# Router fed from the transposed layer result, paired ring slots, and 44 matmuls on constants behind the mixer

## Chip, cores and metric

One core of one Trainium2 chip. The metric is the device time of one execution in microseconds (us). The kernel before takes 895.5 us (median of 3 runs, 894.67 to 897.81). All matrices are float32.

## What is computed

One layer (DEPTH 1) on 320 tokens (256 of a prompt, 64 of 8 samples), model width 2048, 16 experts of width 512 in 4 groups:

```python
def token_mixer(x, ...):
    h = einsum('btd,de->bte', x, w_in)                 # 2048 -> 4352 columns
    b_gate, c_gate, h_conv, u, v, p = split(h, cuts)
    y_conv = b_gate * short_conv(c_gate * h_conv)      # causal, width 3
    y_chunk = u * chunk_mix(layer_norm(v), w_s, b_s)
    y_pool = pool_w(trailing_mean(p) - p) * pool_scale
    return einsum('bte,ed->btd', concat(y_conv, y_chunk, y_pool), w_out)
x = layer_norm(ALPHA * x + token_mixer(x))             # its argument is z below
# router: group logits x @ rg_w (4), expert logits x @ re_w (16); one group, two of its four experts
a = silu(x @ w_gate[e]) * (x @ w_up[e]) * combine[e]
x = layer_norm(ALPHA * x + sum_e a @ w_down[e])
```

## The kernel before, in words

The program is written for the five engines by hand, with semaphores; each engine runs its list in order, and SyncE (SP) issues nearly all loads.

**Mixer.** Both projections run in chunks of 8 x 128 rows by 256 columns of weights (1 MB): 34 chunks of `w_in` (17 groups of two), then 16 of `w_out` (groups 17 to 24, `G_O` = 17), 50 in all (`CHUNKS1`). A chunk c is loaded to `raw[c % 3]`, ScalarE writes its rounded part `w_hi` (`split_hi`), VectorE the remainder `w_lo`, into the place of `raw` (`split_lo`), and TensorE runs 48 matmuls on it (`group_products`) and raises `w_used`. SP issues chunk c when `w_used` is c - 2, so a load has the time of two chunks less the two splits. PSUM holds three pairs of banks, one for each group in turn. The activations stand transposed in SBUF: `xT_hi`, `xT_lo`, later `yT_hi`, `yT_lo` (the latter from `y_lo`, L817). The second half of group 17 waits for the last of these.

**End of the mixer.** For each group k of 256 output columns ScalarE copies the pair of banks to `mixT` (L794), TensorE transposes it back to rows of tokens (`out_tokens`, six transposes, L625 and L630), VectorE adds `ALPHA * x` from `tok` into `tok` (`residual`, L983 and L988) and takes statistics (L997). `store_z` writes `tok` to `z_rows` in DRAM, columns of groups 0 to 5 from ACT's queue, those of 6 and 7 from SP's. After the last group `pe_router` transposes `tok` once more (`turn_z`, L1147, 48 transposes), ScalarE evicts to `zT` (L1370), `route` multiplies it by the router's weights scaled with the norm's gain (L1155), two matmuls on `sums` and `rbias` (L1170, L1171) give the norm's correction, and three with `fold` (L1176) turn the logits to rows. VectorE then works out the selection in small operations (L1460 to L1550), from which come `row` (the first group's tokens; L1464) and `facts`. GpSimd gathers the first expert group's rows from `z_rows` (L1108) when `row` is known and `z_rows` is whole; `info` (L1205) reads `facts`; VectorE builds `order`, `gated` and the next `group_slot` (L1557) and normalises the gathered rows (`xg`, L1589); `fill` (L1220) transposes them, ScalarE evicts with gain and bias (L1390), and `gate_up` (L1284) begins.

**Experts.** Each expert is 6 units of 2 MB: four of gate and up (`gu_w`) and two of down (`down_w`), 96 in all. Units 0 to 4 are loaded during the mixer (`load_half`), units 5 to 10 in `sp_experts` between the mixer's end and the first `gate_up`; every later one, from 11 (`FIRST`), waits for `ring_used`, which TensorE raises with each unit it has used; `gate_up(0, 0)` is the first. SP's list is in order, and so are its loads. At the end comes the last group's norm and its scatter.

## Time and profile before

| | |
|---|---|
| median of 3 runs | 895.5 us |
| profiled execution: device time | 897.55 us |
| profiled execution: span of its instructions | 895.7 us |
| PE busy | 838.7 us, 94% |
| DVE, ACT, POOL busy | 282.4, 263.8, 24.8 us |
| DMA | 267.80 MB, mean 299 GB/s |
| mean granted TensorE clock | 0.979 of 2.4 GHz |

The span is cut by the profile into 40 slices of 22.4 us; the mixer is the first 17.6 of them, the router's stage about 1.5, the experts the rest. "PEld" is TensorE's weight load, "SPq" is SP's queue of DMA issues. A row of a timeline gives the start, the duration, the engine with its line in the kernel, the tiles written and read, and the count where rows were merged; in square brackets the idle time of that engine just before and what ended it. float32 matmuls show twice in a count.

### The profile page before, as it was taken

What the parts mean: (1) busy time and instruction counts of PE and PEld (TensorE: products, weight loads), DVE (VectorE), ACT (ScalarE), POOL (GpSimd) and SP (SyncE); (2) the same over time, 40 slices, a digit from 0 to 9 for tenths busy, and PEclk for the clock granted to TensorE, in tenths of its full rate; (3) what the DMA queues carried; (4) which work ended last, traced back from release to release, by engine and by line L of the source; (5) the groups of instructions that cost most, each with busy time, mean ns of one, the idle gap of its engine ahead of it and who ended that gap; (6) DMA issues with size and microseconds to landing.
All of it is one profiled execution on the core that took longest, in us unless ns stands there. A gap on an engine that the chain in (4) does not pass through costs nothing.

```text
span 895.7 us, 11202 instructions
## 1 busy us (share of the span) xinstructions
PE 838.7 (94%) x4729; PEld 558.7 (62%) x4729; DVE 282.4 (32%) x390; ACT 263.8 (29%) x465; POOL 24.8 (3%) x41
## 2 busy tenths in 40 slices
PE   6999999999999999995989999999999998897993
PEld 6989999999999999983433334433333333333331
DVE  6273384434764435355000102043003220022203
ACT  5234232322233323312432332432223322133101
POOL 0000000000001000001000000000000100000000
PEclk8999999999999999996899999999999999999997
DMA  9643553665444774459898999999999999999980
GB/s 298 185 142 120 188 164 127 192 205 164 144 140 153 282 282 141 141 220 384 353 426 351 421 423 422 428 418 423 424 425 420 424 426 420 422 424 425 421 355 37
DMA packets 81149, 267.80 MB, mean 299 GB/s; under 512 B 5626, under 2 KB 58320, under 8 KB 59657
## 3 DMA queue, kind: packets, MB, share of 16 engines
q1 hardware_dynamic: 78042, 258.92, 74.6%
q0 software_dynamic: 1984, 5.31, 1.5%
q10 hardware_dynamic: 1078, 2.94, 1.0%
q8 instruction: 33, 0.54, 0.2%
q14 instruction: 12, 0.09, 0.0%
HBM read 263.07 MB, written 11.54 MB: 307 GB/s over the span
## 4 chain that ended last, share of the span: by engine, by line
PE 68%; DMA 18%; DVE 6%; ACT 3%; SPq 2%; issue 2%; POOL 0%; POOLq 0%; ACTq 0%; DVEq 0%
PE ps L1284 16%; PE ps L476 12%; PE ps L477 12%; PE ps L478 12%; DMA gu_w<-in_expert_w_up 7%; PE ps L1318 6%; DMA down_w<-in_expert_w_down 4%; DMA xg<-z_rows,row 3%; PE ps L1220 3%; DMA out<-xg,sample_row 3%; SPq L398 2%; ACT xT L1390 1%; PE ps L529 1%; DVE xg L1639 1%; PE ps L1261 1%
## 5 line engine op out<-in xcount | busy, mean ns | idle before, releaser
L1284 PE MATMUL ps<-gu_w,xT 128*64 128x512 f32 x1024 | 235.3, 601 | 14.7 <-DMA gu_w<-in_expert_w_up 13.7
L657 DVE TENSOR_TENSOR w_lo<-raw,w_hi 128x2048 fp32r<-128x2048 f32 x50 | 114.5, 2291 | 173.5 <-ACT w_hi L649 171.9
L1284 PEld LDWEIGHTS ps<-gu_w,xT 128*64 128x64 f32 x1024 | 72.6, 138 | 142.5 <-issue 136.4
L476 PE MATMUL ps<-xT_hi,w_hi 128*128 128x320 f32 x512 | 159.2, 311 | 0.0
L477 PE MATMUL ps<-xT_lo,w_hi 128*128 128x320 f32 x512 | 158.3, 309 | 0.0
L478 PE MATMUL ps<-xT_hi,w_lo 128*128 128x320 f32 x512 | 158.2, 309 | 0.0
L649 ACT ACTIVATE w_hi<-raw 128x2048 fp32r<-128x2048 f32 x49 | 93.8, 1915 | 210.0 <-DMA raw<-in_w_in 138.1
L1390 ACT ACTIVATE xT<-ps,gbT 128x64 f32<-128x64 f32 x256 | 82.2, 406 | 158.7 <-PE ps L1220 158.7
L1318 PE MATMUL ps<-down_w,aT 128*64 128x512 f32 x480 | 106.5, 596 | 0.6
L1661 DVE TENSOR_TENSOR a_sb<-ps,a_sb 128x256 f32<-128x256 f32 x16 | 6.8, 424 | 289.4 <-ACT a_sb L1444 289.4
L476 PEld LDWEIGHTS ps<-xT_hi,w_hi 128*128 128x128 f32 x512 | 96.1, 188 | 0.5
L477 PEld LDWEIGHTS ps<-xT_lo,w_hi 128*128 128x128 f32 x512 | 96.1, 188 | 0.0
L478 PEld LDWEIGHTS ps<-xT_hi,w_lo 128*128 128x128 f32 x512 | 96.1, 188 | 0.0
L476 PE MATMUL ps<-yT_hi,w_hi 128*128 128x320 f32 x256 | 79.8, 312 | 0.9 <-DVE yT_lo L817 0.9
L478 PE MATMUL ps<-yT_hi,w_lo 128*128 128x320 f32 x256 | 79.1, 309 | 0.0
L477 PE MATMUL ps<-yT_lo,w_hi 128*128 128x320 f32 x256 | 79.1, 309 | 0.0
L1318 PEld LDWEIGHTS ps<-down_w,aT 128*64 128x64 f32 x480 | 33.0, 137 | 69.9 <-issue 59.3
L1220 PEld LDWEIGHTS ps<-order,xg 128*128 128x128 f32 x256 | 33.8, 195 | 54.3 <-issue 47.1
L1220 PE MATMUL ps<-order,xg 128*128 128x128 f32 x256 | 45.6, 304 | 5.4 <-DVE xg L1589 5.4
L476 PEld LDWEIGHTS ps<-yT_hi,w_hi 128*128 128x128 f32 x256 | 48.1, 188 | 1.2 <-DVE yT_lo L817 1.1
L477 PEld LDWEIGHTS ps<-yT_lo,w_hi 128*128 128x128 f32 x256 | 48.1, 188 | 0.0
L478 PEld LDWEIGHTS ps<-yT_hi,w_lo 128*128 128x128 f32 x256 | 48.1, 188 | 0.0
(261 smaller groups left out, 523.4 us busy)
## 6 DMA issues: line engine op xcount, KB each, us to landing
gu_w<-in_expert_w_gate SPq DMA_DIRECT2D x64, 1024.0 KB, 15.3
gu_w<-in_expert_w_up SPq DMA_DIRECT2D x64, 1024.0 KB, 19.0
down_w<-in_expert_w_down SPq DMA_DIRECT2D x32, 2048.0 KB, 24.1
raw<-in_w_in SPq DMA_DIRECT2D x34, 1024.0 KB, 5.3
raw<-in_w_out SPq DMA_DIRECT2D x16, 1024.0 KB, 5.4
tok<-in_x_prompt SPq DMA_DIRECT2D x2, 1024.0 KB, 6.0
z_rows<-tok ACTq DMA_DIRECT2D x2, 768.0 KB, 4.1
tok<-in_x_sample SPq DMA_DIRECT2D x1, 512.0 KB, 9.1
```

Source lines behind the costliest of these rows:

```text
L398: sp.dma_start(gu_w[s][:, n, :].rearrange("p (c f) -> p c f", c=4), src[:, e, h, c:c + 4, :])\
L476: pe.matmul(out, wh[:, t, col], hi[:, kt, :], start=(n == 0 and t == 0), stop=False)
L477: pe.matmul(out, wh[:, t, col], lo[:, kt, :], start=False, stop=False)
L478: last = pe.matmul(out, wl[:, t, col], hi[:, kt, :], start=False, stop=(n == 1 and t == CK - 1))
L529: last = pe.transpose(ps[:, n % 8, P * t:P * t + m], tok[0:m, i, 4 * q + t::KT], ident[0:m, 0:m])
L649: act.activation(w_hi[k][:, :], raw[k][:, :], ACT.Copy).then_inc(hi_ready, 1)
L657: dve.tensor_tensor(w_lo[k][:, :], raw[k][:, :], w_hi[k][:, :].bitcast(FP32), ALU.subtract)\
L1220: last = pe.transpose(ps[:, fill_bank(e, j), P * c:P * (c + 1)], xg[g % 2][:, col:HD * (j // 2 + 1):HK], order[:, k, :])
L1261: last = pe.matmul(ps[:, ACC + 2 * h + q, :], gatedT[half, k, :], y[half, 512 * q:512 * (q + 1)], start=(k == 0), stop=(k == EG - 1))
L1284: last = pe.matmul(ps[C * side:C * (side + 1), GU, :], x, w[:, :, c, FH * side:FH * (side + 1)], start=(j == 0 and c == 0), stop=(j == PAI ...
L1318: last = pe.matmul(ps[C * side:C * (side + 1), out + q, :], turned[:, f % 2, f // 2, :], down_w[slot(i)][:, n, col:col + 512], start=(f == ...
L1390: last = act.activation(xT[e % 2][:, j, c, :], ps[:, fill_bank(e, j), P * c:P * c + C], ACT.Identity, bias=gbT[:, 1, j // 2, hc:hc + 1], s ...
```

## The change

Buffers: `raw`/`w_lo` and `w_hi` of a ring slot now lie side by side, so that a slot is one 16 KB piece, and expert units take other places; `slot_at` names them. The rows of `w_in` and of x's transposes are taken as `(t p)` instead of `(p t)`, as those of `w_out` are.

Result: `mixT`, `out_tokens`, `residual`, `turn_z`, the eviction to `zT` and `store_z` go. GpSimd adds `xT_hi` and `xT_lo` into `x_all` (four operations of 128 x 1280, from `w_used` 34). VectorE makes `zt = ALPHA * x_all + ps` (`make_zt`), transposed, and both the router (`route`, for groups 0 to 5 inside the output projection) and the transposes to rows (`rows_of`, in the middle of the next group) read it. ScalarE copies the rows to `z_part` (`copy_rows`) and stores each group's 256 columns itself (`store_rows`); statistics come from `z_part` (`row_sums`). The last group's second half runs column by column. The router's weights are loaded by SP behind chunk 8 in the `(t p)` order, the norm's gain and bias with single elements as runs, and `router_weights` runs in group 18.

Loads: units 5, 6 and 7 are issued at `w_used` 48, `zt_ready` 7 and `w_used` 49, units 8 and 9 at `w_used` 50, unit 10 as before behind `raw_made` and the second `xg` clear.

TensorE: `keep_busy` issues 14, 3, 3, 9 and 15 matmuls 128x128 on `ident` and `slots` into a bank that nobody reads, at five places behind the mixer. The two copies of `vrstd` and `norm_bias` to `facts` move behind `gexp_in`.

```diff
...
-    RING_HI = RAW0 + 24 * KB
-    EARLY0 = RING_HI + 24 * KB
+    EARLY0 = RAW0 + 48 * KB
...
-    raw = [at(f"raw{s}", RAW0 + s * 8 * KB, [P, CH]) for s in range(3)]
-    slot_at = [EARLY0, EARLY0 + 16 * KB, T0 + 32 * KB, T0, T0 + 16 * KB, RAW0 + 16 * KB, RAW0 + 32 * KB,
-               YT_HI0 + 22 * KB, TOK0, RAW0, XA + 24 * KB]
+    raw = [at(f"raw{s}", RAW0 + s * 16 * KB, [P, CH]) for s in range(3)]
+    slot_at = [EARLY0, EARLY0 + 16 * KB, TOK0, TOK0 + 16 * KB, TOK0 + 32 * KB, RAW0 + 32 * KB, XA, RAW0,
+               YT_HI0 + 22 * KB, RAW0 + 16 * KB, XA + 24 * KB]
...
+    x_all = at("x_all", XA, [P, KT, NTOK])
+    zt = [at(f"zt{s}", LATE + s * 2 * ROW, [P, 2, NTOK]) for s in range(3)]
+    z_part = [at("z_part0", XA + 4 * XT_B, [P, 3, GW]), at("z_part1", XA + XT_B, [P, 3, GW])]
...
-    win_v = w_in[0].rearrange("(p t) n -> p t n", t=KT)
+    win_v = w_in[0].rearrange("(t p) n -> p t n", p=P)
...
+            if c == 8:
+                sp.wait_ge(x_full, 12)
+                sp.dma_start(rg_nat[:, :, :], rg_w[0].rearrange("(t p) n -> p t n", p=P)).then_inc(rw_in, 16)
+                sp.dma_start(re_nat[:, :, :], re_w[0].rearrange("(t p) n -> p t n", p=P)).then_inc(rw_in, 16)
+                for k, src in enumerate((ln1_g, ln1_b)):
+                    sp.dma_start(gb_nat[:, k, :], src[0].rearrange("(t p) -> p t", p=P),
+                                 allow_slow_non_contiguous=True).then_inc(gb_nat_in, 16)
+            if c in (12, 16, 20, 24, 28, 32):
...
-            if 4 <= o < 10:
-                if o == 4:
-                    sp.wait_ge(w_used, 2 * G_O)
+            if 6 <= o < 10:
                 if o == 6:
                     sp.wait_ge(ylo_ready, 7)
                     sp.wait_ge(small_out, 16 * (4 + NB))
-                load_half(sp, 2 + (o - 4) // 2, o % 2)
+                    sp.wait_ge(sums_ready, 2)
+                load_half(sp, 3 + (o - 6) // 2, o % 2)
...
+        if free:
+            pe.wait_ge(*free)
...
+            if n and by_column:
+                for f in range(2):
+                    out, col = ps[:, 2 * pair + f, 0:NTOK], slice(P * f, P * (f + 1))
+                    for t in range(CK):
+                        kt = CK * halves[n] + t
+                        pe.matmul(out, wh[:, t, col], hi[:, kt, :], start=False, stop=False)
+                        pe.matmul(out, wh[:, t, col], lo[:, kt, :], start=False, stop=False)
+                        last = pe.matmul(out, wl[:, t, col], hi[:, kt, :], start=False, stop=(t == CK - 1))
+                    last.then_inc(w_used if f else first_column, 1)
+                continue
...
-        def out_tokens(k, turn=0):
...
+        def route(tiles):
+            for kt in tiles:
+                j = kt % RQ
+                last = pe.matmul(ps[RP * j:RP * (j + 1), LGB, 0:NTOK], rw[:, kt, :], zt[kt // 2 % 3][:, kt % 2, :],
+                                 start=(kt < RQ), stop=(kt >= KT - RQ))
+            return last
+        def rows_of(k, columns):
+            for f in columns:
+                pe.wait_ge(zt_ready, k + 1 + (f if k == 7 else 0))
+                if f == 0:
+                    if k == 0:
+                        wait_read(pe, "z0", "z1")
+                    else:
+                        pe.wait_ge(rows_read, 3 * k)
+                for i in range(2):
+                    pe.transpose(ps[:, ROWB, GW * i + P * f:GW * i + P * (f + 1)],
+                                 zt[k % 3][:, f, P * i:P * (i + 1)], ident[:, :])
+                out, samples_of = ps[64 * f:64 * (f + 1), 2 * ((G_O + k) % 3), NTOK:NTOK + P], zt[k % 3][:, f, SEQ:NTOK]
+                if f == 0:
+                    last = pe.transpose(out, samples_of, ident[:, :])
+                else:
+                    last = pe.matmul(out, samples_of, ident[:, :], start=True, stop=True)
+            return last
+        def behind(k):
+            def step(n):
+                if n != CK - 1:
+                    return
+                rows_of(k, (0, 1)).then_inc(rows_made, 1)
+                if k % 2:
+                    if k == 1:
+                        pe.wait_ge(rw_ready, 4)
+                    route(range(2 * k - 2, 2 * k + 2)).then_inc(zt_used, 1)
+                if k == 6:
+                    pe.wait_ge(sums_ready, 2)
+                    pe.wait_ge(rbias_in, 32)
+                    out = ps[:, 3, 0:2 * NR]
+                    pe.matmul(out, ones[:, :].bitcast(FP32), sums[:, :, :].rearrange("p k n -> p (k n)"),
+                              start=True, stop=False)
+                    pe.matmul(out[:, NR:2 * NR], ones[0:1, :].bitcast(FP32), rbias[:, :], start=False, stop=True)\
+                      .then_inc(both_made, 1)
+            return step
 
         pe.wait_ge(ylo_ready, 4)
         group_products(pe, G_O, Y, HALF_O, wait_half=(ylo_ready, 7))
-        with pe.Fori(0, 2) as s:
-            for i in range(3):
-                group_products(pe, G_O + 1 + i, Y, HALF_O, s, 3)
-                out_tokens(i, s)
-        group_products(pe, G_END - 1, Y, HALF_O)
-        out_tokens(6)
-        out_tokens(7)
+        for k in range(1, 8):
+            group_products(pe, G_O + k, Y, HALF_O, between=behind(k - 1), by_column=(k == 7),
+                           free=(zt_ready, k - 2) if k >= 3 else None)
+        rows_of(7, (0,))
+        route(range(KT - 4, KT - 1))
+        rows_of(7, (1,)).then_inc(rows_made, 1)
+        route(range(KT - 1, KT)).then_inc(lgT_made, 1)
...
-    def store_z(eng, k, cols):
...
+    def copy_rows(act, k):
+        act.wait_ge(rows_made, k + 1)
+        if k == 1:
+            act.wait_ge(x_whole, 4)
+        if k >= 2:
+            act.wait_ge(z_stored[k % 2], 32 * (k // 2))
+            act.wait_ge(rows_seen, k - 1)
+        part = z_part[k % 2]
+        act.activation(part[:, 0:2, :], ps[:, ROWB, :].rearrange("p (i c) -> p i c", i=2), ACT.Copy).then_inc(rows_read, 1)
+        for f in range(2):
+            act.activation(part[0:64, 2, P * f:P * (f + 1)], ps[64 * f:64 * (f + 1), 2 * ((G_O + k) % 3), NTOK:NTOK + P],
+                           ACT.Copy).then_inc(rows_read, 1)
+    def store_rows(act, k):
+        act.wait_ge(rows_read, 3 * (k + 1))
+        col, part = slice(GW * k, GW * (k + 1)), z_part[k % 2]
+        act.dma_start(z_dram[0:SEQ, col].rearrange("(i p) c -> p i c", p=P), part[:, 0:2, :]).then_inc(z_stored[k % 2], 16)
+        act.dma_start(z_dram[SEQ:NTOK, col], part[0:64, 2, :]).then_inc(z_stored[k % 2], 16)
...
-        def copy_out_group(k, turn=0):
...
+        for k in range(6):
+            split_hi(act, 2 * (G_O + k) + 4)
+            copy_rows(act, k)
+            store_rows(act, k)
+            if k == 0:
+                act.wait_ge(x_whole, 4)
+                act.dma_start(rbias[:, 0:NG], rg_b[0:1, :]).then_inc(rbias_in, 16)
+                act.dma_start(rbias[:, NG:NG + NE], re_b[0:1, :]).then_inc(rbias_in, 16)
+            split_hi(act, 2 * (G_O + k) + 5)
+        copy_rows(act, 6)
+        store_rows(act, 6)
+        copy_rows(act, 7)
...
-        def residual(k, turn=0):
...
+        def router_weights():
+            dve.wait_ge(rw_in, 32)
+            dve.wait_ge(gb_nat_in, 32)
...
+        def make_zt(k, columns=slice(0, 2)):
+            pair = (G_O + k) % 3
+            if k == 0:
+                dve.wait_ge(x_whole, 4)
+            if k >= 3:
+                dve.wait_ge(zt_used, (k - 3) // 2 + 1)
+            a, b = columns.start, columns.stop
+            last = dve.scalar_tensor_tensor(out=zt[k % 3][:, columns, :], in0=x_all[:, 2 * k + a:2 * k + b, :],
+                                            scalar=ALPHA, in1=ps[:, 2 * pair + a:2 * pair + b, 0:NTOK],
+                                            op0=ALU.mult, op1=ALU.add)
+            last.then_inc(zt_ready, 1)
+        def row_sums(k):
+            part = z_part[k % 2]
+            dve.wait_ge(rows_read, 3 * k + 1)
+            for i in range(2):
+                steps.inc(dve.bn_stats(xstats[:, i, k, :], part[:, i, :]))
+            dve.wait_ge(rows_read, 3 * k + 3)
+            dve.bn_stats(xstats[0:64, 2, k, :], part[0:64, 2, :]).then_inc(rows_seen, 1)
+        for k in range(8):
+            c = 2 * (G_O + k) + 2
+            if c < CHUNKS1:
+                split_lo(dve, c)
+            if k:
+                row_sums(k - 1)
+            if k < 7:
+                dve.wait_ge(w_used, c)
+                make_zt(k)
+            else:
+                dve.wait_ge(first_column, 1)
+                make_zt(7, slice(0, 1))
+                dve.wait_ge(w_used, CHUNKS1)
+                make_zt(7, slice(1, 2))
+            if c + 1 < CHUNKS1:
+                split_lo(dve, c + 1)
+            if k == 0:
+                router_weights()
+        row_sums(7)
...
-        sp.wait_ge(w_used, CHUNKS1)
-        order = [EARLY, EARLY + 1, SLOTS, EARLY + 2, SLOTS + 1, SLOTS - 1] + list(range(FIRST, len(ORDER)))
-        for i in order:
+        for i in range(EARLY, len(ORDER)):
             e, u = ORDER[i]
             s = slot(i)
-            if i == SLOTS:
-                store_z(sp, 8, slice(6 * GW, 8 * GW))
-            if i == SLOTS - 1:
-                sp.wait_ge(z_stored, 16 * 6)
-                sp.wait_ge(zT_full, 12)
-            if i == SLOTS + 1:
+            if i == EARLY:
+                sp.wait_ge(w_used, CHUNKS1 - 2)
+            elif i == EARLY + 1:
+                sp.wait_ge(zt_ready, 7)
+            elif i == EARLY + 2:
+                sp.wait_ge(w_used, CHUNKS1 - 1)
+            elif i == EARLY + 3:
+                sp.wait_ge(w_used, CHUNKS1)
+            elif i == FIRST - 1:
...
+        pool.wait_ge(w_used, 2 * G_O)
+        for q in range(4):
+            four = slice(4 * q, 4 * q + 4)
+            pool.tensor_tensor(x_all[:, four, :], xT_hi[:, four, :].bitcast(FP32), xT_lo[:, four, :].bitcast(FP32),
+                               ALU.add).then_inc(x_whole, 1)
...
+        pool.wait_ge(rows_seen, 7)
+        pool.wait_ge(z_stored[0], 32 * 4)
         pool.memset(xg[0][:, :], 0.0).then_inc(xg_zero, 1)
-        pool.wait_ge(z_stored, 16 * 6)
-        pool.wait_ge(zT_full, 12)
+        pool.wait_ge(rows_seen, 8)
+        pool.wait_ge(z_stored[1], 32 * 4)
...
+    def keep_busy(pe, n):
+        for _ in range(n):
+            pe.matmul(ps[:, 2, 0:P], ident[:, :], slots[:, :], start=True, stop=True)
...
-        turn_z(0)
-        turn_z(1)
-        pe.wait_ge(rw_ready, 4)
-        route(0)
...
+        keep_busy(pe, 14)
...
+        keep_busy(pe, 3)
...
+        keep_busy(pe, 3)
...
+        keep_busy(pe, 9)
...
+        keep_busy(pe, 15)
...
-        def turn(n):
-            q, i = divmod(n, 3)
-            t0, m = TILES[i]
-            act.wait_ge(zT_full, n + 1)
-            act.copy(zT[:, 4 * q:4 * q + 4, t0:t0 + m],
-                     ps[:, Z_BANKS[n % 6], :].rearrange("p (t c) -> p t c", t=4)[:, :, 0:m]).then_inc(zT_ready, 1)
-        for n in range(3):
-            turn(n)
+        act.wait_ge(lgT_made, 1)
+        act.copy(lgT[:, 0:NTOK], ps[:, LGB, 0:NTOK]).then_inc(lgT_ready, 1)
+        store_rows(act, 7)
...
```

## Rows read from the trace of the kernel before

**Rows 1.** The page, part 2: 40 equal slices of the span, in tenths.

```profile
PEclk8999999999999999996899999999999999999997
...
DMA  9643553665444774459898999999999999999980
```

**Rows 2.** The chain that ended last: start us, us, what.

```profile
415.40 8.54 DMA xg<-z_rows,row
...
427.33 5.63 PE ps L1284 x16
...
434.49 3.58 PE ps L1284 x16
...
837.24 33.28 DMA down_w<-in_expert_w_down
```

**Rows 3.** A window: busy us (x) of each engine, PEclk, DMA share, GB/s.

```profile
430.00:435.00 5.00, 5.00 (x28) 2.40 (x26) 0.00 (x0) 1.35 (x5) 0.00 (x0) 0.86 0.42 133
```

**Rows 4.** SP's queue in order of time: start us, us, what.

```profile
394.41 0.34 SPq L398 DMA_DIRECT2D gu_w<-in_expert_w_gate  x1
...
433.01 0.33 SPq L398 DMA_DIRECT2D gu_w<-in_expert_w_gate  x1
```

**Rows 5.** TensorE's waits before 394 us: total, times, longest.

```profile
PE ps L476 <- DVE yT_lo L817: 0.9, 1, 0.9
```

**Rows 6.** SP's queue in the output projection, loads of w_out.

```profile
306.01 0.37 SPq L424 DMA_DIRECT2D raw<-in_w_out  x1
...
313.71 0.37 SPq L424 DMA_DIRECT2D raw<-in_w_out  x1
...
320.75 0.37 SPq L424 DMA_DIRECT2D raw<-in_w_out  x1
```

**Rows 7.** The timeline from 398 to 425 us, DVE and PE, columns as before.

```profile
398.06 1.07 DVE L997 BATCH_NORM_STATS2 xstats<-tok 128x6 f32<-128x256 f32 x3
...
401.03 0.16 DVE L1037 SCALAR_TENSOR_TENSOR norm_bias<-vmv,vrstd 128x3 f32<-128x3 f32 x1
...
406.83 0.41 PE L1170 MATMUL ps<-sums,ones 128*128 128x40 f32 x2
...
407.49 0.74 PE L1155 MATMUL ps<-zT,rw 128*32 128x320 f32 x8
...
409.74 0.22 DVE L1460 TENSOR_TENSOR logits<-ps,vrstd 128x60 f32<-128x60 f32 x1 [1.43 <-PE ps L1176]
...
419.00 0.15 DVE L1550 TENSOR_SCALAR row_no<-token 128x1 f32<-128x1 f32 x1
...
422.48 0.55 DVE L1557 TENSOR_TENSOR group_slot<-slots,group_rank 128x384 fp32r<-128x384 f32 x1
...
423.97 1.53 DVE L1589 TENSOR_SCALAR xg<-xg,told 128x1024 f32<-128x1024 f32 x2 [0.94 <-DMA xg<-z_rows,row]
```

**Rows 8.** The groups of PE by line: busy us, mean ns | idle us.

```profile
L592 PE MATMUL ps<-wsT,vtok 128*128 128x128 f32 x24 | 3.6, 273 | 0.0
```

**Rows 9.** The timeline of DVE around 280 us.

```profile
277.40 2.29 DVE L657 TENSOR_TENSOR w_lo<-raw,w_hi 128x2048 fp32r<-128x2048 f32 x1 [5.72 <-ACT w_hi L649]
...
283.72 0.82 DVE L817 TENSOR_TENSOR yT_lo<-tmp,yT_hi 128x640 fp32r<-128x640 f32 x1 [0.81 <-ACT yT_hi L681]
```

**Rows 10.** The timeline of POOL at 25 us.

```profile
25.25 0.86 POOL L450 TENSOR_SCALAR_AFFINE_SELECT ws_nat<-ws_nat 128x768 f32<-128x768 f32 x1 [22.28 <-DMA wsb_nat<-in_sgu_w]
```

**Rows 11.** SP's queue from 62 us, then ACT at 80 us.

```profile
62.31 0.37 SPq L416 DMA_DIRECT2D raw<-in_w_in  x1
...
74.80 16.29 SPq L416 DMA_DIRECT2D raw<-in_w_in  x3
...
79.97 1.91 ACT L649 ACTIVATE w_hi<-raw 128x2048 fp32r<-128x2048 f32 x1 [4.54 <-DMA raw<-in_w_in]
```

**Rows 12.** Two windows from 16 us, columns as in Rows 3.

```profile
16.00:19.00 3.00, 3.00 (x12) 3.00 (x12) 2.41 (x2) 2.40 (x2) 0.00 (x0) 0.50 1.10 347
...
19.00:23.50 4.50, 4.50 (x24) 4.50 (x24) 3.80 (x2) 1.91 (x1) 0.00 (x0) 0.69 1.16 254
```

217 lines of the change are left out of this document (60 added, 157 removed).

## The prediction

> **What bounds the kernel now.** I read the slices first, then the chain, then the queue of loads. The granted clock is at full through the mixer, falls only in the two slices of the router's stage, and is back to full after; DMA is partly busy in the mixer and full in nearly every slice behind it [rows 1]. So there are two bounds in turn: TensorE until about 394 us, the stream of expert weights afterwards. The chain ends with 33 us on one load of down weights [rows 2]: at the end TensorE waits for bytes, and making it faster there buys nothing.
>
> What does buy time is the moment from which the stream runs without a hole. Units 5 to 10 are issued between 394.41 and 419 us. Unit 11 waits for the first unit used, so SP issues it at 433.01, just when `gate_up(0, 0)` ends (427.33 + 5.63 = 432.96) [rows 2, 4]. Before that DMA had run dry: its share in 430 to 435 us is 0.42 [rows 3]. At that moment all of units 0 to 10 but the one used lie in SBUF, before and after the change alike, and everything later (85 units, the gathers, the ring) hangs on it. So I forecast the end by the shift of one event, the end of `gate_up(0, 0)`. That units 5, 6 and 7 are loaded up to 14 us earlier buys nothing by itself: the ring is full sooner, and DMA idles longer before unit 11.
>
> **Part 1: TensorE's work before the mixer ends.** Call the last release of a `w_out` chunk T; it is 394.4 before [rows 4]. TensorE waits only 0.9 us in this stretch [rows 5], so work added there lengthens it one for one. A chunk with six transposes takes 7.70 us, one without 7.04: 0.66 us for `out_tokens` [rows 6]. `rows_of` has five transposes (0.55) and one plain float32 matmul of 3.6/12 = 0.30 us [rows 8]: 0.85. Six `out_tokens` become seven `rows_of` before T: 7 x 0.85 - 6 x 0.66 = 2.0. Three calls of `route` move ahead of T, at 0.7 each (L1155, [rows 7]): 2.1. The two matmuls on `sums` and `rbias` fill 406.83 to 407.49: 0.7 [rows 7]. Sum 4.8, T = 399.2. The waits of `rows_of` and `route` find `zt` seven us old, and DVE and ACT have room in the output projection: nothing. `router_weights` is some 3 us of small DVE work in group 18, inside its idle time.
>
> **Part 2: GpSimd's four adds.** They start at `w_used` 34 (about 276 us) and so run beside the only tight place of the mixer: DVE's chain from `w_lo` at 277.40 to the last `yT_lo` at 284.54, for which TensorE waits 0.9 us [rows 5, 9]. No row of before has GpSimd and DVE at work together there. The lower bound is nothing. The upper: GpSimd passes 768 elements in 0.86 us [rows 10], so 1280 with two inputs are 1.4 to 2.9 us; if each add and each DVE subtraction with both inputs in SBUF excluded one another, `w_lo` would start at 278.9 and each of the two `yT_lo` wait behind a further add; the last would end near 288.4 at 2.9 us an add (+3.9) and near 284.8 at 1.4 (+0.3). I take 2, between them.
> The Trainium skill ("GPSIMD Engine Reference", 3.1 Elementwise — side-by-side cycle accounting) measures 4497 ns for such an add of 2048 elements: an estimate of 2.8 us for 1280, at which exclusion would cost about 3.8 and the sum below would be -2.4. No row here shows GpSimd on two inputs.
>
> **Part 3: the small loads behind chunk 8.** The four loads of router weights, gain and bias are cut into 4 x 2048 runs of 4 to 64 bytes: 512 for each of 16 DMA engines, on the queue in which chunk 9 follows. Chunk 8 is issued at 62.31 and lands 5.2 us later (as chunk 9 does, 74.80 to 79.97); chunk 9's products begin when the third release of that row comes, 74.80 + 16.29 - 0.37 = 90.7 [rows 11]. Less 1.9 and 2.3 us for its splits and 5.2 to land, chunk 9 must reach the head of the queue by 81.3. From 66.3 (chunk 8 off the queue) that leaves 15 us, or 29 ns for a run. A price for small runs: from 19 us, when eight loads of 48 runs each are in flight, DMA moves 254 GB/s with its engines full instead of 347 [rows 12]. (347 - 254) / 347 x 4.5 us x 16 / 384 = 50 ns, an upper end, since other loads and completions lie in it; the lower is no loss. At 50 ns the stall is 10.6 us. I take 30 ns: +0.6.
>
> **Part 4: from T to the first `gate_up`.** All from [rows 2, 7]. The second column's `zt` takes about 0.4 us (half a 128x640 row), hidden by `rows_of` and `route` of the first. The last `route` starts at T + 1.4. Before, 2.25 us pass from there (407.49) to the logits (409.74), with lgT's copy and the `fold` matmuls; now lgT's copy stands behind three copies of rows, 0.6 more: raw logits T + 4.3. The other branch is later: rows copied T + 2.8, statistics T + 3.35, then 2.06 to `norm_bias` (399.13 to 401.19) T + 5.4, three operations of 0.22 to the offset. Logits start at T + 6.2 (before: T + 15.3). The 48 transposes and 12 evictions are what is saved.
> From logits to the gather's issue 5.66 + 0.3 (the two copies moved in): T + 12.15. GpSimd also waits for the last `z_rows` store, issued about T + 4 and landing by T + 10. The chain to `row_no` is 9.3 + 0.3, less 0.4 for matmuls at full clock: ends T + 15.6. From there to the end of `group_slot` (423.03) were 3.9, now 3.0: T + 18.6. The gather took 8.54 us under load; now units 5 to 9 (25 us of stream from T - 13.9) are nearly through, so 6.5 to 8.5: T + 18.7 to 20.7. Half of the normalising, 0.8: T + 19.5 to 21.5.
> `keep_busy`: a matmul is 0.30 us [rows 8]. Blocks 14, 3, 3, 9 are 4.2, 0.9, 0.9, 2.7 us; the first ends at T + 8.5, 0.7 past `member`'s groups, but DVE has its own operations until T + 9.4; the others end within their waits. The 15 (4.5 us) run from T + 16.2 to T + 20.7 and stand before `fill`. So `fill` starts at about T + 21.2. Then 2.2 to `gate_up` (2.5 before, at half clock), and 3.6 instead of 5.63 if the clock holds: T + 27.0, where it was T + 38.6.
>
> **Sum.** 399.2 + 27.0 = 426.2, against 432.96: -6.8. With +2.0 and +0.6: -4.2. Span 895.7 - 4.2 = 891.5. The profiled run's device time is 897.55, 2.05 above the median of the runs; I apply the difference to the median: 895.5 - 4.2 = 891.3.
>
> **Rivals.**
> *Both doubtful terms are nothing.* The adds don't disturb DVE and the small runs fit their room: -6.8, 888.7. For it: no row shows a disturbance of either kind that is sure. Against: the adds start 1.4 us before `w_lo` [rows 9], so they do meet, and the windows show a loss by small runs [rows 12].
> *The adds and DVE's subtractions exclude one another.* The upper end of part 2, +3.9 instead of 2: -2.3, 893.2. The sign is in the place: two `yT_lo`, each behind an add. The Trainium skill ("SBUF — State Buffer", Who interferes with whom) states this as a rule: a VectorE instruction with two SBUF inputs and a GpSimd instruction that reads SBUF block each other for a whole instruction. No trace here shows it so far.
> *The small loads hold chunk 9 (slower).* The mechanism of part 3 at 50 ns a run: 25.6 us against 15 of room, +10.6 with +2 and -6.8: +5.8, 901.3. It turns to a loss from 29 + 4.8/512 = 39 ns. Speaking for it, the windows; against, that these contain more than the runs.
> *The 44 matmuls don't do what they are for, or stand in the way.* The clock still falls: gate_up +2.0, info and fills +1: -1.2, 894.3. Against: the clock was full until about 410 us in spite of short waits.
>
> **How the numbers follow.** Forecast 0.38, both nothing 0.2, exclusion 0.2, small loads 0.12, clock 0.1. 0.3% is 2.7 us, about what a measurement of this kernel can tell. Faster: most of the forecast, all of the second, under half of the third and a little of the last, 0.65; within 0.3%: 0.2; slower: 0.15, the small loads and what I overlook in a change of this size. Range 885.5 to 899.5: below, both terms nothing and a gather that lands in 5 us with a transposed chain 1 us shorter; above, the small loads at about 46 ns.
>
> **What would show each step.** `w_used` 50 at T = 399 if parts 1 to 3 hold; TensorE's waits before T say which of 2 and 3 was missed (before `L476` at 284 us, or at 90 us in group 4). Logits 6 us behind T and the gather 12 us behind it; the clock at full from T to `gate_up`; SP's issue of unit 11 near 429; after that the same distances as before to the end. I would be wrong most simply if the end didn't move with unit 11's issue.

## The result, and the profile after

The changed kernel takes 900.4 us (median of 9 runs, 898.2 to 902.1) against 896.5 for the kernel before (9 runs beside them): a ratio of 1.0041, 95% interval 1.0028 to 1.0054. It is slower by 0.4%, outside the range of the prediction, and on the side to which I gave 0.15. The profiled execution has a span of 900.2 us and a device time of 902.11 us, the longest of the nine; the rows of this section are from it.

The page's slices (PEclk: granted clock in tenths; DMA: busy share in tenths) answer [rows 1]. The clock now falls at two places: once in the mixer, near 285 us, where it was full before, and in the router's stage as before.

```profile
PEclk9999999999998999998999999999999999999997
DMA  9655553655464486587799999999999999999980
```

The windows put numbers to both (us, PE busy and instructions, granted clock, DMA share, GB/s). At 285 us the clock is at half (1.2 of 2.4 GHz) for some 6 us (0.59 and 0.73 in the two windows); in the router's stage it is at half from about 419 to 429, in spite of the matmuls on constants.

```profile
285.00:290.00 5.00, 3.07 (x11) 0.59 0.48 163
290.00:295.00 5.00, 5.00 (x27) 0.73 0.04 3
...
415.00:420.00 5.00, 3.81 (x24) 0.90 0.71 275
420.00:425.00 5.00, 5.00 (x25) 0.50 0.19 35
425.00:430.00 5.00, 5.00 (x27) 0.58 0.87 342
```

SP's queue answers [rows 4] and [rows 6]:

```profile
319.08 0.37 SPq L436 DMA_DIRECT2D raw<-in_w_out  x1
...
327.90 0.37 SPq L436 DMA_DIRECT2D raw<-in_w_out  x1
...
334.94 0.37 SPq L436 DMA_DIRECT2D raw<-in_w_out  x1
...
405.85 0.81 SPq L1142 DMA_DIRECT2D down_w<-in_expert_w_down  x2
...
436.18 0.33 SPq L403 DMA_DIRECT2D gu_w<-in_expert_w_gate  x1
```

A chunk with `rows_of` and a `route` takes 8.82 us, one with neither 7.04, one with `rows_of` alone 8.15. The last `w_out` chunk is released at T = 405.85 (394.4 before, 401.8 by the prediction's sum), unit 11 is issued at 436.18 (433.01 before, 428.8 predicted).

What is late in the mixer stands in the timelines around 280 us (start, duration, what; in brackets the idle time ahead and its releaser); they answer [rows 9] and [rows 5]:

```profile
274.82 14.83 POOL L1155 TENSOR_TENSOR x_all<-xT_hi,xT_lo 128x1280 f32<-128x1280 f32 x4 [247.22 <-PE ps L502]
...
277.75 5.00 POOL L1155 TENSOR_TENSOR x_all<-xT_hi,xT_lo 128x1280 f32<-128x1280 f32 x1
...
275.26 4.67 DVE L708 TENSOR_TENSOR w_lo<-raw,w_hi 128x2048 fp32r<-128x2048 f32 x1 [4.61 <-ACT w_hi L700]
...
281.47 1.96 DVE L869 TENSOR_TENSOR yT_lo<-tmp,yT_hi 128x640 fp32r<-128x640 f32 x1 [0.81 <-ACT yT_hi L744]
...
285.09 1.78 DVE L869 TENSOR_TENSOR yT_lo<-tmp,yT_hi 128x640 fp32r<-128x640 f32 x1 [0.80 <-ACT yT_hi L744]
286.96 4.84 DVE L708 TENSOR_TENSOR w_lo<-raw,w_hi 128x2048 fp32r<-128x2048 f32 x1
...
286.93 0.64 PE L500 MATMUL ps<-yT_hi,w_hi 128*128 128x320 f32 x1 [4.50 <-DVE yT_lo L869]
```

GpSimd's four adds cover 275 to 290 us. In that time VectorE's subtractions with two inputs in SBUF take about twice as long: `w_lo` 4.67 and 4.84 us instead of 2.29, `yT_lo` 1.96 and 1.78 instead of 0.82. TensorE waits 4.5 us for the last `yT_lo` instead of 0.9.

The ends of these rows show how the time is lost: the two engines take turns, one whole instruction at a time. The first add ends at 277.78, and the `w_lo` that stands in the trace from 275.26 ends 2.15 us behind it, at 279.93. The second add (from 277.75) ends at 282.75, 2.82 us behind that `w_lo`. The `yT_lo` of 281.47 ends at 283.43, 0.68 behind the second add. Each ends about its undisturbed time (2.29, 2.96 and 0.82 us) after the other's end.

And the router's stage, against [rows 7]:

```profile
410.53 1.07 DVE L876 TENSOR_SCALAR vstd<-vmv 128x3 f32<-128x3 f32 x1
...
417.73 0.16 DVE L1502 TENSOR_SCALAR row<-ps 128x1 int32<-128x1 f32 x1
...
421.79 0.15 DVE L1588 TENSOR_SCALAR row_no<-token 128x1 f32<-128x1 f32 x1
...
409.78 1.80 POOL L1172 MEMSET xg<- 128x2048 f32 x1 [117.55 <-DMA z_rows<-z_part]
422.51 1.12 POOL L1179 DMA_INDIRECT xg<-z_rows,row  x1 [10.94 <-DMA z_rows<-z_part]
...
419.66 4.21 PE L1210 MATMUL ps<-slots,ident 128*128 128x128 f32 x18
423.66 1.40 PE L1251 MATMUL ps<-facts,group_slot 128*128 128x11 f32 x6
424.98 5.63 PE L1210 MATMUL ps<-slots,ident 128*128 128x128 f32 x30
...
432.49 3.65 PE L1330 MATMUL ps<-gu_w,xT 128*64 128x512 f32 x16 [1.00 <-ACT xT L1427]
```

`row` is ready at 417.73, but the gather is issued at 422.51. `row_no` is ready at 421.79, but TensorE is inside its block of 9 until 423.87 and starts `info` only then. The block of 15 takes 5.6 us and ends at 430.6; `fill` follows.

### The profile page after: what moved, and what is told of

The parts are those of the page before. It is cut to its first block, busy times and chain, and to the rows that moved or that the text cites. A ratio compares the mean times of both kernels' runs of the same rounds, so it can differ in the third digit from the quotient of the medians.

```text
span 900.2 us, 11218 instructions
## 1 busy us (share of the span) xinstructions
PE 847.4 (94%) x4777; PEld 565.7 (63%) x4777; DVE 288.1 (32%) x383; ACT 260.9 (29%) x469; POOL 38.8 (4%) x43
## 4 chain that ended last, share of the span: by engine, by line
PE 74%; DMA 13%; DVE 4%; SPq 3%; ACT 3%; issue 1%; POOLq 0%; POOL 0%; ACTq 0%
PE ps L1330 19%; PE ps L500 12%; PE ps L502 11%; PE ps L501 11%; PE ps L1364 9%; DMA gu_w<-in_expert_w_up 7%; DMA down_w<-in_expert_w_down 4%; PE ps L1266 3%; SPq L403 3%; ACT xT L1427 1%; DMA raw<-in_w_in 1%; PE ps L1210 1%; PE ps L1307 1%; DVE w_lo L708 1%; PE ps L527 1%
## 5 line engine op out<-in xcount | busy, mean ns | idle before, releaser
L708 DVE TENSOR_TENSOR w_lo<-raw,w_hi 128x2048 fp32r<-128x2048 f32 x50 | 119.4, 2389 | 141.3 <-ACT w_hi L700 139.2
L700 ACT ACTIVATE w_hi<-raw 128x2048 fp32r<-128x2048 f32 x49 | 93.8, 1915 | 211.2 <-DMA raw<-in_w_in 138.0
L500 PE MATMUL ps<-yT_hi,w_hi 128*128 128x320 f32 x240 | 76.3, 318 | 4.5 <-DVE yT_lo L869 4.5
L1364 PEld LDWEIGHTS ps<-down_w,aT 128*64 128x64 f32 x480 | 33.1, 137 | 69.8 <-issue 59.5
L501 PE MATMUL ps<-yT_lo,w_hi 128*128 128x320 f32 x240 | 75.4, 314 | 0.0
L502 PE MATMUL ps<-yT_hi,w_lo 128*128 128x320 f32 x240 | 75.4, 314 | 0.0
L500 PEld LDWEIGHTS ps<-yT_hi,w_hi 128*128 128x128 f32 x240 | 46.1, 192 | 6.9 <-DVE yT_lo L869 4.8
L501 PEld LDWEIGHTS ps<-yT_lo,w_hi 128*128 128x128 f32 x240 | 46.1, 192 | 0.0
L502 PEld LDWEIGHTS ps<-yT_hi,w_lo 128*128 128x128 f32 x240 | 46.1, 192 | 0.0
```

What stands on the lines that cost most here:

```text
L500: pe.matmul(out, wh[:, t, col], hi[:, kt, :], start=(n == 0 and t == 0), stop=False)
L501: pe.matmul(out, wh[:, t, col], lo[:, kt, :], start=False, stop=False)
L502: last = pe.matmul(out, wl[:, t, col], hi[:, kt, :], start=False, stop=(n == 1 and t == CK - 1))
L700: act.activation(w_hi[k][:, :], raw[k][:, :], ACT.Copy).then_inc(hi_ready, 1)
L708: dve.tensor_tensor(w_lo[k][:, :], raw[k][:, :], w_hi[k][:, :].bitcast(FP32), ALU.subtract)\
L1364: last = pe.matmul(ps[C * side:C * (side + 1), out + q, :], turned[:, f % 2, f // 2, :], down_w[slot(i)][:, n, col:col + 512], start=(f == ...
```

## Experiments

T is the release of the last `w_out` chunk; where SP issues nothing at it, I take the start of the last `rows_of`, 0.2 us earlier in the changed kernel, plus 0.2. T, the issue of unit 11 and the span are those of one profiled execution of each kernel, whose device time lies up to 2.4 us from the median of its runs (e7: 887.3 against 889.7).

| kernel | T | unit 11 issued | T to unit 11 | span | device median | ratio to before |
|---|---|---|---|---|---|---|
| before | 394.4 | 433.0 | 38.6 | 895.7 | 896.5 | 1 |
| changed | 405.9 | 436.2 | 30.3 | 900.2 | 900.4 | 1.0041 [1.0028, 1.0054] |
| e1 adds on VectorE | 399.0 | 427.6 | 28.6 | 892.1 | 893.5 | 0.997 [0.9948, 0.9991] |
| e2 no matmuls on constants | 406.3 | 435.6 | 29.4 | 900.7 | 901.0 | 1.0052 [1.0032, 1.0071] |
| e3 filled wait | 402.9 | 431.9 | 28.9 | 894.3 | 896.8 | 1.0006 [0.9991, 1.0021] |
| e4 e2, downs late | 406.2 | 436.1 | 29.9 | 900.8 | 900.7 | 1.0041 [1.0026, 1.0057] |
| e5 e1, loads behind gather, blocks fitted | 398.8 | 425.3 | 26.5 | 890.4 | 891.4 | 0.9935 [0.9919, 0.9952] |
| e6 e5 without the matmuls | 397.4 | 425.7 | 28.3 | 890.9 | 892.5 | 0.995 [0.9934, 0.9967] |
| e7 e5, one down first, transposes | 395.4 | 422.0 | 26.6 | 885.4 | 889.7 | 0.9929 [0.991, 0.9949] |
| e8 adds after the low parts | 399.5 | 428.2 | 28.7 | 891.2 | 893.2 (one run) | |
| e9 e7, blocks fitted again | 396.1 | 421.0 | 24.9 | 884.0 | 888.2 | 0.9913 [0.9897, 0.9929] |
| e10 e1, first block longer | 397.7 | 426.8 | 29.1 | 890.9 | 892.8 (one run) | |
| e11 e1, small loads thrice | 408.4 | 441.6 | 33.1 | 905.8 | 907.8 (one run) | |

The ratios are against runs of the kernel before on the same chip (medians 896.5, 896.9, 896.9 and 895.5 us in the four groups). The start of the kernel varies: chunk 9's load, up to which the code is the same in all of them but the kernel before and e11, is issued between 71.5 and 73.5 us. T carries these up to 2 us along; T to unit 11 doesn't. The granted clock goes with it: it is 1.00 throughout from 13 to 23 us in e6, e7, e8 and e10, where that load is issued at 71.5 to 71.8, and at half for 2 us or more in the rest of these kernels, where it is issued at 72.9 to 73.5.

### Whose fault the long wait in the mixer is: e1, e8

e1 moves the four adds to VectorE:

```
-        for q in range(4):
-            pool.tensor_tensor(x_all[:, four, :], xT_hi[...], xT_lo[...], ALU.add)
+            if k == 0:
+                whole(0)
+                whole(1)
             if c < CHUNKS1:
                 split_lo(dve, c)
+            if k == 0:
+                whole(2)
+                whole(3)
```

> The four adds that make x_all run on VectorE instead of GpSimd, two before and two behind the low part of chunk 36; nothing else differs from the changed kernel. My theory: in the changed kernel GpSimd's adds (274.82 to 289.65 us) stretched VectorE's low parts (w_lo 2.29 to 4.67 us, yT_lo 0.82 to 1.96 and 1.78), TensorE waited 4.5 us for yT_lo instead of 0.9, and the wait made the granted clock fall to half for about 6 us. So here: w_lo 2.29 and yT_lo 0.82 again, the wait at most 0.9 us, the clock full from 280 to 300 us, the last w_out chunk released at about 399.9 instead of 405.9 us, and the span about 5 to 6 us shorter than the changed kernel's 900.2: 894 to 895. Rival: the low parts were late for another reason (ScalarE, the order of loads) and merely overlap with the adds: yT_lo stays late, the wait stays near 4.5 us and the span at 900.

```profile
281.83 0.82 DVE L869 TENSOR_TENSOR yT_lo<-tmp,yT_hi 128x640 fp32r<-128x640 f32 x1 [0.81 <-ACT yT_hi L744]
282.69 2.89 DVE L1076 TENSOR_TENSOR x_all<-xT_hi,xT_lo 128x1280 f32<-128x1280 f32 x2
...
PE ps L500 <- DVE yT_lo L869: 0.5, 1, 0.5
...
285.00:290.00 5.00, 5.00 (x36) 1.00 0.46 154
...
399.04 0.81 SPq L1153 DMA_DIRECT2D down_w<-in_expert_w_down  x2
```

The subtractions are back at 2.29 and 0.82, the wait is 0.5, the clock stays full, T is 6.8 us earlier. VectorE makes an add in 1.48 us and has the time for it. This one edit turns the changed kernel from 0.4% slower into 0.3% faster.

e8 leaves the adds on GpSimd and makes them wait for the last `yT_lo` (`pool.wait_ge(ylo_ready, 7)` moved ahead of them).

> The changed kernel, with GpSimd's four adds moved behind VectorE's last yT_lo (one wait moved up). Theory of exclusion in the shared access to SBUF: the two yT_lo take 0.82 us again, TensorE's wait is 0.9 us or less and the clock stays full there; GpSimd alone needs 2.8 us an add, 11 to 12 us in all from 283, with VectorE's w_lo in that time stretched (2.29 to 4.5 or more). x_all is then whole at about 296, 4 to 5 us behind the release of chunk 36 (291), zt(0) and the low part of chunk 37 wait for it, and TensorE loses about 1 to 2 us there: T near 401 to 402, span 896. Rival: the low parts were late for another reason than the adds: yT_lo stays above 1.7 us.

```profile
281.43 2.97 POOL L1156 TENSOR_TENSOR x_all<-xT_hi,xT_lo 128x1280 f32<-128x1280 f32 x1 [253.27 <-DVE yT_lo L869]
...
284.36 5.01 POOL L1156 TENSOR_TENSOR x_all<-xT_hi,xT_lo 128x1280 f32<-128x1280 f32 x1
...
280.45 0.82 DVE L869 TENSOR_TENSOR yT_lo<-tmp,yT_hi 128x640 fp32r<-128x640 f32 x1 [0.80 <-ACT yT_hi L744]
282.33 4.22 DVE L708 TENSOR_TENSOR w_lo<-raw,w_hi 128x2048 fp32r<-128x2048 f32 x1 [1.05 <-ACT w_hi L700]
```

`yT_lo` is at 0.82 again although GpSimd makes the same four adds: it is their overlap that costs. Alone an add takes 2.96 us; the second, which stands in the trace while `w_lo` has its turn, took 5.01, and `w_lo` 4.22. They take turns here too: the first add ends at 284.40, `w_lo` 2.15 us behind it at 286.55, the second add 2.82 us behind that at 289.37. TensorE loses 1.6 us here, 1.1 for the low part of chunk 37 and 0.5 for `zt`, as expected; that T is 399.5 and not 401 to 402 is the start, 1.8 us earlier than in the changed kernel.

### Whether the clock is a loss of its own: e3

```
             if n and wait_half:
+                pe.wait_ge(pair_free[0], 6)
+                for _ in range(14):
+                    pe.matmul(ps[:, 0, 0:P], ident[:, :], slots[:, :], start=True, stop=True)
                 pe.wait_ge(*wait_half)
```

> The changed kernel with 14 further matmuls on constants (3.4 us at full clock) put where TensorE waits 4.5 us for the last yT_lo (282.4 to 286.9 us), into a bank that is free by then; GpSimd's adds stay. Theory: the fallen clock after that wait is a second loss beside the wait: the wait's end stays at 286.9 us, but with TensorE occupied the clock stays full, the chunk behind it takes 7.04 us instead of 9.9, and everything behind moves forward by about 2.4 us: last w_out chunk released at 403.4, span about 898. Rival: the clock falls for another reason at that place, or 14 matmuls are too few: window 285 to 292 us keeps a granted clock near 0.5 and the span stays at 900.

```profile
284.77 1.78 DVE L872 TENSOR_TENSOR yT_lo<-tmp,yT_hi 128x640 fp32r<-128x640 f32 x1 [0.81 <-ACT yT_hi L747]
...
285.00:290.00 5.00, 3.62 (x26) 1.00 0.42 140
290.00:295.00 5.00, 5.00 (x36) 1.00 0.04 4
```

GpSimd's adds are there, the `yT_lo` is as slow as ever (1.78) and ready at the same time, but TensorE is occupied, the clock stays full, and T is 2.9 us earlier. Counted from the last `yT_lo`, without the start, it is 118.2 us instead of 120.8: the clock was worth 2.6. The wait itself was 3.6 longer than before; the two make the 6.2 us that group 17 lost. Here matmuls on constants did what they are for.

### What the 44 matmuls are worth: e2, e6, e10, e9

e2 leaves out all five blocks.

> The changed kernel without any of the 44 matmuls on constants. Theory that they trade evenly: without them info(0) starts 1.5 us earlier (421.9 instead of 423.45 us) and the first fill up to 1.4 us earlier (about 429), but gate_up(0,0) runs at half clock (5.6 us instead of 3.65), so it ends near 436.6 instead of 436.1 and the span stays within 1 us of 900.2. Rival 1, they stand in the way: the clock in the router's stage falls in either case, gate_up gets its full clock anyhow, and the span is 1.5 to 2 us shorter (898.5). Rival 2, they do what they are for: without them also the small matmuls ahead of the gather run at half clock, and the span is 1.5 us or more longer (902).

From T to unit 11 it takes 29.4 us instead of 30.3, and the medians are 901.0 and 900.4: a difference within 1 us, as the first theory says. Without the blocks `info` starts right at `row_no`, the fill at 428.26 instead of 430.45, and the half clock costs `gate_up(0, 0)` 1.1 us (4.77 instead of 3.65). The gain and the harm about cancel.

e5 and e6 are the same pair after the lengths have been fitted to the waits (20, 6, 4, 12, 6 against none); e5's other edit is told below.

> The same as the kernel whose loads 8 to 10 stand behind the gather, without any matmul on constants. If the matmuls keep the clock: here info(0) takes about 1.5 us instead of 0.9, the first fill 2.0 instead of 1.0 and gate_up(0,0) 4.8 to 5.6 instead of 3.65, so gate_up(0,0) ends 2.5 to 3.5 us later than with them. If they are worth nothing (as the pair with 14, 3, 3, 9, 15 and with none suggested), it ends within 1 us. In the span the difference appears only where unit 11's issue sets the end; where units 8 to 10 are still landing then, the span is the same within 1 us.

With them the clock stays full through the whole stage (1.00 in each window from 400 to 430) and T to unit 11 is 26.5; without them 28.3. The medians differ by 1.1 us, but the intervals of the ratios overlap, so the time itself doesn't show the gain. My 2.5 to 3.5 was too much: `gate_up` recovered its clock in its course (4.70 us, not 5.6).

e10 changes only the first block of e1, from 14 to 20, to close the wait of 1.5 us behind it.

> The kernel with the adds on VectorE, with only the first of the five blocks of matmuls on constants changed: 20 instead of 14. In its trace TensorE waited 1.5 us for member behind that block and the granted clock fell to half 3 to 4 us later, so that the block of 9 took 4.21 us and held info(0) until 417.3, 1.9 us behind row_no. If that wait is what made the clock fall: here the wait is 0.2 us, the clock stays full from 405 to 425, the block of 9 takes 2.2 us, info(0) starts at row_no (T + 16.4), gate_up(0,0) still cannot start earlier than the block of 15 and the gather (landed T + 21) allow, and unit 11 is issued at T + 27 to T + 28 instead of T + 28.55. Rival: the clock falls as before (the many waits of 0.4 to 0.8 us are enough), and nothing changes.

The wait went to 0.5 us and the clock fell all the same (granted 0.51 from 410 to 415 us, against 1.00 in e5), `info` starts 1.9 us behind `row_no`, and T to unit 11 is 29.1. The theory that this one wait was the cause does not hold in this profile. e5 differs in the blocks behind it and in where the loads are issued, and there the clock stayed; which of the remaining waits of 0.2 to 0.8 us decides was not tried. e9 is e7 (below) with the last block 12 long and a block of 3 between the fills and `gate_up(0, 0)`.

> The kernel with one down unit first and the transposed sample rows, with two blocks of matmuls on constants changed: the last one 12 long instead of 6 (ends 0.3 us before the first fill can start, instead of 1.5), and a new one of 3 between the first two fills and gate_up(0,0), where TensorE waited 1.0 us. There gate_up(0,0) ran at half clock (5.35 us); here it takes 3.65, unit 11 is issued 1.5 us earlier from T (T + 24.9 instead of T + 26.6), and the time is about 1.5 us shorter: 888 median. Rival: the clock falls there in some executions and not in others whatever the waits are: no difference.

```profile
410.00:415.00 5.00, 4.99 (x43) 1.00 0.87 323
...
417.31 3.65 PE L1335 MATMUL ps<-gu_w,xT 128*64 128x512 f32 x16 [0.33 <-ACT xT L1433]
...
421.00 0.33 SPq L403 DMA_DIRECT2D gu_w<-in_expert_w_gate  x1
```

T to unit 11 is 24.9 as expected, and 888.2 us is the best median measured, 0.9% under the kernel before. That the block of 3 kept the clock is not shown: the 1.7 us are those by which `gate_up(0, 0)` was shorter, and e5, with waits of 1.73 us ahead of the fill and 1.00 ahead of `gate_up` like those of e7 (1.52 and 0.99), ran it in 3.65 us too. The rival of the expectation stands, and the intervals of e7 and e9 overlap.

### What holds the gather, and whether bytes or TensorE set the end: e4, e5, e7

e4 takes e2 and lets units 8 and 9 wait for the last `z_rows` store:

```
             elif i == EARLY + 3:
-                sp.wait_ge(w_used, CHUNKS1)
+                sp.wait_ge(z_stored[1], 32 * 4)
```

> The changed kernel without the 44 matmuls, and with the loads of units 8 and 9 (down weights) waiting for the landing of the last z_rows store instead of for the last w_out chunk. To be compared with the kernel without the 44 matmuls alone. Theory: in the changed kernel the last store (issued 408.7 and 409.1 us) lies in the DMA engines behind units 8 and 9 (issued 405.85) and holds the gather until 422.51 although its row numbers stand at 417.73. Here the store lands by about 412 us, the gather is issued at about 418.6 and lands in 5.6 to 8.5 us, 1 to 4 us earlier than in the changed kernel (428.1), fill(0,0) starts by about 426.5 to 428, gate_up(0,0) ends 1 to 2.5 us earlier than without this edit, and the span is as much shorter. Rival: the gather is now itself behind units 8 and 9 in the engines and lands no earlier, or the fill is set by the facts and not by the gather: the span is that of the kernel without the 44 matmuls, within 0.7 us.

```profile
418.90 1.12 POOL L1179 DMA_INDIRECT xg<-z_rows,row  x1 [7.24 <-DVE row L1497]
...
428.33 1.54 DVE L1622 TENSOR_SCALAR xg<-xg,told 128x1024 f32<-128x1024 f32 x2 [2.08 <-DMA xg<-z_rows,row]
```

The first half was right: the store lands by 411.6, and the gather goes out at 418.90, 3.1 us earlier than in e2. The second was wrong: units 8 and 9 now lie ahead of the gather itself, it takes 9.4 us to land instead of 5.4, and nothing is won. The rival holds.

e5 puts the three loads behind the gather, on top of e1:

```
             elif i == EARLY + 3:
                 sp.wait_ge(w_used, CHUNKS1)
-            elif i == FIRST - 1:
                 sp.wait_ge(raw_made, 1)
                 sp.wait_ge(xg_zero, 2)
```

> The kernel with the adds on VectorE, and two edits more: units 8, 9 and 10 are all issued behind the first gather's issue (before: 8 and 9 at the last w_out chunk), and the blocks of matmuls on constants are 20, 6, 4, 12 and 6 long instead of 14, 3, 3, 9 and 15, fitted to the waits that the traces show. From the adds-on-VectorE run: last w_out chunk T = 399.0; the last z_rows store lands by about T + 5.5 with no load before it; row numbers T + 11.9, gather issued T + 12.7 = 411.7 instead of 414.97, landed by 417; with the clock at full, info(0) starts at row_no (415.3), normalising at 418.5, fill(0,0) at 419.4, gate_up(0,0) ends at about 425.1 instead of 427.55, and unit 11 is issued then. Theory A, the prediction's rule (the end moves with unit 11's issue): the end moves by -2.4 against the adds-on-VectorE kernel. Theory B, the end is set by bytes: DMA is at its full rate from unit 11 to the last unit, so what counts is how late the bytes are. Units 8 to 10 (6.3 MB, 15 us at 420 GB/s) are issued from about 414.5 and end near 429.5, so unit 11's bytes begin at 429.5 although it is issued at 425.1: the end moves by +2 against the adds-on-VectorE kernel, in which unit 11's bytes begin at 427.6.

The gather is issued at T + 13.1 and normalising is no longer held by it (no idle time ahead of it on VectorE):

```profile
475.00:500.00 25.00, 24.94 (x118) 1.00 0.98 402
...
411.93 1.12 POOL L1185 DMA_INDIRECT xg<-z_rows,row  x1 [7.24 <-DVE row L1508]
...
418.53 1.53 DVE L1633 TENSOR_SCALAR xg<-xg,told 128x1024 f32<-128x1024 f32 x2
```

The same window of e1:

```profile
475.00:500.00 25.00, 24.93 (x120) 1.00 0.84 327
```

Unit 11 is issued 2.3 us earlier than in e1 and the time is 2.0 us shorter (891.4 against 893.5). Theory B, that late bytes cost, asked for +2 and is wrong. The windows show why: after unit 11 there is one more stretch in which DMA is not full, 475 to 500 us. TensorE is busy for 24.9 of these 25 us and waits for nothing; the loads wait for the slots that it releases. In e1 the share is 0.84, in e5 0.98: the bytes that came later were made up there. Up to that place the end hangs on TensorE's own chain, which starts with `gate_up(0, 0)`. e5 has two edits against e1, and they were not timed apart. Of T to unit 11, the place of the loads is worth about 1.1 us (29.4 in e2 and 28.3 in e6, both without blocks) and the blocks 1.8 (e6 against e5).

e7 issues unit 8 when the last store has landed and transposes both columns' sample rows:

```
-                out, samples_of = ps[64 * f:64 * (f + 1), 2 * ((G_O + k) % 3), NTOK:NTOK + P], zt[...]
-                if f == 0:
-                    last = pe.transpose(out, samples_of, ident[:, :])
-                else:
-                    last = pe.matmul(out, samples_of, ident[:, :], start=True, stop=True)
+                out, samples_of = ps[0:64, 2 * ((G_O + k) % 3) + f, NTOK:NTOK + P], zt[...]
+                last = pe.transpose(out, samples_of, ident[:, :])
```

> As the kernel whose loads 8 to 10 stand behind the gather, but unit 8 is issued as soon as the last z_rows store has landed, 9 and 10 behind the gather; and the second column's sample rows in rows_of are transposed into the second bank of the pair instead of multiplied by the identity as a plain float32 matmul. Part 1 of the prediction: a w_out chunk with rows_of alone took 8.15 us against 7.04 without, 1.11 for it; with a sixth transpose in place of the matmul (six transposes cost 0.66 in the kernel before) it should take 7.04 + 0.66 = 7.7, and T move by 7 x 0.45 = -3.1 if the whole excess is the plain matmul's; rival: the excess is in changing banks and weights, and the chunk stays at 8.0 or more. Theory B on bytes: unit 8 lands before the gather is issued, 9 and 10 need 10 us from T + 15.5, so they end at T + 25.5 and unit 11, issued at T + 26, finds the engines just free: with T = 396 to 397 its bytes begin near 422.5, the end is 5 us earlier than with the adds on VectorE alone: about 888. By theory A it is the same; against the kernel with all three behind the gather theory B says 7 us, theory A 3 us.

```profile
319.26 0.37 SPq L436 DMA_DIRECT2D raw<-in_w_out  x1
...
326.31 0.37 SPq L436 DMA_DIRECT2D raw<-in_w_out  x1
...
334.00 15.97 SPq L436 DMA_DIRECT2D raw<-in_w_out  x3
...
416.57 5.35 PE L1335 MATMUL ps<-gu_w,xT 128*64 128x512 f32 x16 [0.99 <-ACT xT L1432]
```

A chunk with neither takes 7.05 (319.26 to 326.31), one with `rows_of` alone 7.69 (to 334.00) instead of 8.15: there the whole excess was the plain matmul's. Where a `route` follows, the gain is smaller (8.56 in e9, which has the same code, instead of 8.82). Over seven calls that is 2.5 us, not 3.1; the rest of the 3.4 by which T is earlier than in e5 is the start. T to unit 11 is the same as in e5 (26.6 and 26.5), and so theory A and B can't be told apart by this run: unit 11 is issued 3.3 us earlier, the span is 5.0 shorter, the median 1.7. In this profile `gate_up(0, 0)` ran at half clock (5.35 us); in e9's it took 3.65. That hides a gain ahead of it: the fill starts at T + 19.0 instead of T + 20.6, and 1.1 us of that is `vstd`, which takes 0.17 us here because GpSimd's memset of `xg` starts behind it, and 1.25 in e5.

### The price of small loads: e11

> The kernel with the adds on VectorE, with the four small loads behind chunk 8 made three times (the two further sets into memory that nobody reads): 24576 runs of 4 to 64 bytes instead of 8192, 1536 for each of the 16 DMA engines instead of 512. This prices the slower rival of the prediction. At my price of 30 ns a run they take 46 us, at 19 ns (what issue and landing in the changed kernel's trace allow at most: 61.4 to 71.1 us for 512) 29 us from 61: chunk 9 lands at 95.6, its products begin at 100 instead of 89.5, so TensorE waits 10 us. If only SP's issuing counts (7 us a set, 21 us in all): chunk 9 is issued at 82.5, its products begin at 92, a wait of 2 to 3 us. The span is longer by the wait.

```profile
68.00:72.00 4.00, 4.00 (x29) 1.00 1.00 45
72.00:76.00 4.00, 4.00 (x29) 1.00 0.97 49
76.00:80.00 4.00, 4.00 (x30) 1.00 0.92 43
80.00:84.00 4.00, 1.11 (x10) 0.97 0.99 211
...
PE ps L609 <- ACT wsT L745: 6.8, 1, 6.8
```

In e1, with one set:

```profile
68.00:72.00 4.00, 4.00 (x30) 1.00 0.70 43
72.00:76.00 4.00, 4.00 (x29) 1.00 0.35 94
```

With one set the engines are full of small runs until about 71 us, with three until about 82: 11 us for 1024 further runs on each engine, about 11 ns a run, not 30. SP spends the same 10.8 us (68.46 to 79.21) on issuing the two further sets, so the run does not tell which of the two sets the pace; 11 ns is the price of a run either way. At that price one set needs 6 us of the 15 that are free. With three sets SP issues chunk 9 at 79.26, and TensorE's wait is 6.8 us, not for chunk 9 itself but for `wsT`: ScalarE's copy of it stands in order behind the high part of chunk 9. T is 9.4 us later than in e1; the clock is at half from 84 to 94. It is at half again in the router's stage, where the block of 15 took 6.3 us, and T to unit 11 is 33.1. Both numbers of my expectation, 10 and 2 to 3, were off.

## Why the prediction was wrong

The step that failed most is part 2: the adds beside VectorE were put at +2.0 us and cost +6.2. Of the 7.3 us by which unit 11 came later than forecast, 4.2 are this term, 3.3 the stage from T to `gate_up` (part 4) and 1.7 TensorE's added work (part 1); the small loads and an earlier start give 1.9 back.

The ledger, in us against the kernel before, for the issue of unit 11:

| term | predicted | measured |
|---|---|---|
| first stage | 0 | -1.3 |
| part 1, TensorE's work before T | +4.8 | +6.5 |
| part 2, adds beside VectorE | +2.0 | +6.2 |
| part 3, small loads | +0.6 | 0 |
| part 4, T to `gate_up`'s end (38.6 before) | -11.6 | -8.3 |
| sum | -4.2 | +3.1 |

**What bounds the kernel.** The rule held: the span less the issue of unit 11 is 462.4 to 465.2 us in all thirteen kernels, 462.7 before and 464.0 after, so the end moves with that issue, within 1.3 us between these two and within 2.8 us over all. My reason for it was half of the truth. I said that the stream has no hole after unit 11. It has one at 475 to 500 us (it shows as the 8 of the slice from 470 to 493 us in [rows 1]; I read over it), and up to there TensorE's chain sets the pace; the bytes set it behind.

**Part 1** was mis-sized by 1.7. From the issue at w_used 38 to T there are 88.4 us before (306.01 to 394.41) and 93.8 after (312.04, read from the two loads grouped at 303.90 to 312.41, to 405.85), +5.4, and 1.1 for the first `rows_of`. `rows_of` costs 1.11, not 0.85: I had priced the plain matmul at 0.30 from [rows 8], where 12 of them run in a row; here the step with it costs 0.46 more than with a transpose, where no `route` follows (e7: 7.69 instead of 8.15).

**Part 2** was the large error. The rival (exclusion) had the mechanism and the price of the wait: +3.9 predicted for it, 4.5 instead of 0.9 measured, which is +3.6. I gave the forecast a 2 between nothing and that, as a mean of two cases of which one had to be true. The Trainium skill's rule ("SBUF — State Buffer", Who interferes with whom) was stated for just this pair of instructions, and e1 and e8 bear it out: two SBUF inputs on VectorE against GpSimd's adds, while VectorE's multiplications with an input in PSUM (`tmp`, 0.81 and 0.82) were untouched in the same stretch. It holds in the size too: a 0.82 us subtraction lasted 1.96 and 1.78 us because it met an add under way and waited for the rest of it, not for a whole further add. The estimate of 2.8 us for an add, from the Trainium skill's "GPSIMD Engine Reference" (3.1 Elementwise — side-by-side cycle accounting), came close as well: alone it takes 2.96. What neither my forecast nor any rival had in this place is the second half: the wait of 4.5 us took the clock along, 2.6 us by e3.

**Part 3.** No wait shows up. The price of a run was 50 ns as upper end, 30 taken and 11 measured. (My sum was also off: 512 runs at 30 ns are 15.4 us against 15 of room, +0.4 and not +0.6, and no row gives the 66.3 us from which I counted the room; by [rows 11] chunk 8 lands at 67.5.) The windows from which I took 50 held other loads and completions, as I wrote; I should not have gone as far from the lower end.

**Part 4.** Logits start at T + 7.2 instead of 6.2: `vstd` takes 1.07 us instead of 0.17 beside GpSimd's memset of `xg` (409.78 to 411.58), and 0.17 in e7 and e9, where the memset starts behind it. The row numbers come at T + 11.9, as said. The gather is issued at T + 16.7 and not at T + 12.15: I had let the last store land by T + 10, issued 408.7 and 409.1 behind two units of 2 MB of 405.85, and they took up to 12.6 us to land. `row_no` at T + 16.1 was right within 0.5 (my own terms add up to 15.4, not 15.6). Then the block of 9 held `info` for 1.5 us and the block of 15 held `fill` for 1.4 us, both stretched by the clock that they were to keep; fill at T + 24.6 instead of 21.2. Without the blocks the late gather alone would have let it start at about T + 23.2 (an estimate: the normalising at 428.15 and 0.86 us from there to the fill, as in e5), so 2.0 of the 3.4 us are the gather's and 1.4 the blocks'. From there to the end of `gate_up` 5.7, as predicted (5.8). In e1, e3 and e8 the same stage takes 28.6 to 28.9, with GpSimd's adds (e3, e8) or without: there the block of 15 ran at full clock (3.62 us instead of 5.63); with loads and blocks in order (e9) 24.9, less than the 27.0 of the prediction.

**The first stage.** Chunk 9's load is issued 1.3 us earlier than before (73.51 against 74.80), and up to 3.3 us earlier in the other kernels of this family, which share its code up to there. The clock's half stretch at 15 to 22 us is shorter there (0.66 against 0.50 in 15 to 20 us, 1.00 against 0.82 in 20 to 25). In e6, e7, e8 and e10 the stretch is absent, and chunk 9 is issued another 1.7 to 2.0 us earlier. So this term goes with the clock; what keeps or lowers the clock there was not tested, and I had costed the new order of `w_in`'s rows at nothing. I had read the clock as full through the mixer, though the first slice of [rows 1] is an 8.

**The rivals.** Both terms nothing: the small loads yes, the adds no. Small loads hold chunk 9: not at one set; at three they do. The 44 don't do what they are for: right about the clock (half from about 419 to 429), and the sign of their net effect is open in the changed kernel. Only the rival of the small loads reached 900 (901.3), and its mechanism did not occur. It took exclusion with its clock, a dearer `rows_of` and the held gather together. The slower end of my range rested on the small loads, the one term that came out at nothing.

## What to carry to other kernels

Work handed to an idle engine is not free if its instructions and those of the engine on the critical path must take turns, as GpSimd's adds and VectorE's subtractions with two SBUF inputs did: put it where that engine is idle, or on that engine if its own price is lower (1.48 us against 2.96 here). A wait of some us on TensorE can cost twice, once by itself and once by the clock behind it (4.5 and 2.6 us here). Matmuls on constants paid where they filled most of a wait that could not be avoided (e3), and did harm where they stood ahead of work that was ready; fitted to the many short waits of the router's stage they made the stage 1.8 us shorter, which the times of e5 and e6 do not separate. Before a load is issued early, see what small transfer must pass through the same engines next.

## What the hardware did that I had not expected

- GpSimd and VectorE took turns by whole instructions, and either could be the one that waits: an add of 128x1280 took 2.96 us alone and 5.01 with the turn of a `w_lo` in it, and that `w_lo` 4.22 instead of 2.29. It held for small instructions too: a 3-element `vstd` took 1.07 us instead of 0.17 and ended at 411.60, with the memset (411.58); in e1 GpSimd's cast of 3 elements took 2.11 us instead of 0.19 and ended at 287.84, with VectorE's `w_lo` (287.79).
- The clock was at half from 286 to 292 us, behind one wait of 4.5 us in a stretch of dense matmuls; with 3.4 us of that wait filled it never fell.
- Whether it falls is not fixed by the program: the mean granted clock of e1 was 0.981 in the run of 897.9 us and 0.991 in that of 890.3. And behind the same wait of 1.8 us for `xT` near 460 us the granted clock was 1.00 from 450 to 475 in the kernel before, in the changed one and in e9, and 0.93 in e1 and e5; it cost e1 1.7 us of its lead (unit 11 was 5.4 us ahead of the kernel before, the load issued at 467.88 3.7).
- A gather of 1 MB took 8.5 us to land under load before, 9.4 us in e4 behind units 8 and 9, 5.4 to 5.7 in the changed kernel, e1, e2 and e8, and 5.8 to 6.6 in e5, e6, e7 and e9. The last stores to `z_rows` took 10.0 to 12.6 us behind units 8 and 9 (the changed kernel, e1, e2, e3, e8), and 2.2 to 2.6 with no load issued ahead of them (e5, e6, e7, e9).
